# Running the stage ahead of each norm in two token halves, with the first half's norm steps issued inside the second half

## The reference

```python
h = h + (gate_a * ya + gate_b * yb) @ w_out                  # first model: two attentions
h = h + memory_cross_attn(rms_norm(h), rms_norm(mem), ...)
h = h + conv_gated_mlp(rms_norm(h), w_up, ..., w_down)       # 1024 -> 2*2816 -> 1024
x = rms_norm(h)                                              # ln_f: its result is the second model's input

# second model, each sublayer f: h = h + rms_norm_post(f(rms_norm_pre(h)))
#   layer 0: swiglu, gmlp_mixer, swiglu, embedding
#   layer 1: swiglu, rwkv7_mixer, swiglu, embedding
swiglu(x)    = (silu(x @ w1) * (x @ w3)) @ w2                 # D_FF 2816
embedding(x) = sigmoid(x @ w_gate) * (p @ w_proj)             # p: 512 x 256
rms_norm(x)  = x * rsqrt(mean(x*x, axis=-1) + 1e-6) * g
```

## Time and profile before

| | |
|---|---|
| median of 3 runs | 4235.42 us (4219.64 to 4237.18) |
| the profiled execution's own time | 4230.84 us |
| its span, first to last instruction | 4229.0 us |
| mean granted TensorE clock | 0.889 of full speed |
| busy: TensorE 87%, VectorE 44%, ScalarE 28% | of the span |
| HBM read / written | 279.07 MB / 2.10 MB |

### The profile page before, as it was taken

The page is one execution under the profiler, slowest core; times in us unless marked ns, Lnnn a source line. Parts: engine busy times, 40 slices in busy tenths (PEclk is TensorE's granted clock), DMA queues, the critical chain, the costliest instruction groups (busy, mean ns, idle before and its releaser), DMA issues. The chain is left out here.

```text
span 4229.0 us, 50513 instructions
## 1 busy us (share of the span) xinstructions
PE 3670.3 (87%) x22482; PEld 2958.7 (70%) x22482; DVE 1851.5 (44%) x2268; ACT 1167.1 (28%) x1423; POOL 0.2 (0%) x4
## 2 busy tenths in 40 slices
PE   7888579779998999869899978999687677689996
PEld 6656357658877887868788867887466666478874
DVE  5222223547734333454433244333646774743334
ACT  2222432332222222323322223222333231232222
POOL 0000000000000000000000000000000000000000
PEclk9758789869998999889899988999888987789997
DMA  3001012202222222212122311222120000012221
GB/s 134 30 0 60 0 50 100 70 30 100 93 90 77 100 84 95 100 50 100 60 100 88 102 65 60 100 85 66 62 78 28 3 3 12 31 69 100 85 90 40
DMA packets 43273, 284.40 MB, mean 67 GB/s; under 512 B 4785, under 2 KB 4913, under 8 KB 16817
## 3 DMA queue, kind: packets, MB, share of 16 engines
q1 hardware_dynamic: 43056, 281.18, 19.3%
HBM read 279.07 MB, written 2.10 MB: 66 GB/s over the span
## 5 line engine op out<-in xcount | busy, mean ns | idle before, releaser
L392 PE MATMUL ps<-xh,wh 128*128 128x512 f32 x2688 | 1065.2, 396 | 68.1 <-DVE xl L1502 33.9
L392 PE MATMUL ps<-xl,wh 128*128 128x512 f32 x2688 | 1059.6, 394 | 0.0
L392 PE MATMUL ps<-xh,wl 128*128 128x512 f32 x2688 | 1058.2, 394 | 0.0
L289 DVE TENSOR_TENSOR wl<-raw,wh 128x2048 fp32r<-128x2048 f32 (+3 forms) x284 | 591.6, 2083 | 557.7 <-ACT wh L284 556.7
L392 PEld LDWEIGHTS ps<-xh,wh 128*128 128x128 f32 x2688 | 511.7, 190 | 202.2 <-issue 83.5
L284 ACT CAST wh<-raw 128x2048 fp32r<-128x2048 f32 (+3 forms) x284 | 493.0, 1736 | 417.8 <-PE ps L392 412.6
L392 PEld LDWEIGHTS ps<-xh,wl 128*128 128x128 f32 x2688 | 511.3, 190 | 110.0 <-issue 1.5
L392 PEld LDWEIGHTS ps<-xl,wh 128*128 128x128 f32 x2688 | 512.3, 191 | 107.8 <-issue 0.8
L392 PE MATMUL ps<-hid_h,wh 128*128 128x512 f32 x880 | 347.1, 394 | 1.1 <-DVE wl L289 1.1
L392 PE MATMUL ps<-hid_h,wl 128*128 128x512 f32 x880 | 347.0, 394 | 0.0
L392 PE MATMUL ps<-hid_l,wh 128*128 128x512 f32 x880 | 347.0, 394 | 0.0
(11 more groups left out here) (301 smaller groups left out, 4025.8 us busy)
## 6 DMA issues: line engine op xcount, KB each, us to landing
raw<-in_up SPq DMA_DIRECT2D x88, 1024.0 KB, 4.9
raw<-in_down SPq DMA_DIRECT2D x64, 704.0 KB, 4.1
raw<-in_up_c SPq DMA_DIRECT2D x22, 1024.0 KB, 4.9
raw<-in_down_c SPq DMA_DIRECT2D x16, 704.0 KB, 4.0
raw<-in_gates SPq DMA_DIRECT2D x8, 1024.0 KB, 4.8
raw<-in_gv SPq DMA_DIRECT2D x8, 1024.0 KB, 4.9
raw<-in_gu SPq DMA_DIRECT2D x8, 1024.0 KB, 4.9
raw<-in_gout SPq DMA_DIRECT2D x8, 1024.0 KB, 4.9
```

The costliest lines, as they stand in the source:

```text
L289: nc.vector.tensor_tensor(wl[:, slot, 0:w], raw[:, slot, 0:w], wh[:, slot, 0:w].bitcast(F32), ALU.subtract).then_inc(lo_ready, 1)
L392: last = nc.tensor.matmul(out, stationary, moving, start=(fresh and q == 0), stop=(t == kt - 1 and half == per - 1 and q == 2), skip_group ...
```

## The change

The stages `down_c`, `down_00`, `down_01`, `down_10`, `down_11`, `gout`, `rout` and `ple_gate0/1` each run twice, as `...a` on tokens 0 to 255 and `...b` on tokens 256 to 511. Each half streams, casts and subtracts all the stage's weight chunks again. The stages behind the norms (`up_*`, `gv`, the rwkv inputs) stay whole.

A `Chain` holds the two passes of one token half as 12 numbered steps. `Chain(0)` is handed to stage b as `along`: at every hook (one a chunk in `down_*`, two a chunk in `gout`, `rout` and `ple_gate`) each engine issues its part of the next step, in line with the stage's own instructions: behind the split of the next chunk on ScalarE and VectorE, behind the chunk's matmuls on TensorE. What is left (`rest()`), and all of `Chain(1)`, is issued behind stage b, ahead of the next stage. In a chain the second pass's squares are added by VectorE and not by TensorE.

`embed` now runs `ple_proj` first (the split of `p` is made a whole feed-forward earlier), with `Chain(1)` of the norm ahead as its `along` and that of `ple_gate_a`; `ple_gate_b` carries `Chain(0)` of the next norm. The output leaves in two DMAs.

Everywhere a unit has at most two output tiles: `branch_a`, `branch_b`, `xo`, `lora_w2`, `lora_a2`, `lora_g2` and `ple_proj` evict two at a time where they evicted four, from 4 banks of PSUM by turns.

```diff
+def by_halves(name, width, count):
+    return [(name + "a", name, width, range(count)), (name + "b", name, width, range(count))]
...
+STREAM += stage("up_00", 2048, KF) + by_halves("down_00", DOWN, 2 * KD)
+STREAM += stage("gv", 2048, 8) + stage("gu", 2048, 8) + by_halves("gout", 2048, 8)
...
     def linear(...,
+               tokens=EVERY, last_rows=P, norms=None, sums=False, along=None):
+        hooks = max(1, blocks * kt // 8)
...
         @block.vector
         def _(dve):
...
+            for unit in range(units):
+                for half in range(per):
+                    n = a + unit // lots * per + half + 1
+                    if unit % lots == 0 and n < len(order):
+                        split_lo(dve, n, n % 2, order[n][2])
+                    if along:
+                        for _ in range(hooks):
+                            along.dve(dve, hook)
+                            hook += 1
+                if dve_part:
+                    wait_products(dve, unit)
+                    dve_part(dve, unit, outputs(unit), side(unit))
...
+    class Chain:
+        SUM, ROOT, APPLY, SUM_2, ROOT_2, WRITE, END = 0, 1, 2, 5, 6, 7, 12
+        def pe(self, pe, step):
+            if step == self.SUM:
+                self.one.sum_up(pe)
+            elif step == self.ROOT:
+                self.one.spread(pe)
+            elif step == self.SUM_2 and self.two:
+                self.two.sum_up(pe)
+            elif step == self.ROOT_2 and self.two:
+                self.two.spread(pe)
+        def act(self, act, step):
+            if step == self.ROOT:
+                self.one.square_root(act)
+            elif self.APPLY <= step < self.APPLY + 4 and self.two:
+                for t in range(2 * (step - self.APPLY), 2 * (step - self.APPLY) + 2):
...
+                    self.two.square(act, t, self.one)
...
+            elif self.WRITE <= step < self.WRITE + 4 and self.two and self.two.split:
+                for t in range(2 * (step - self.WRITE), 2 * (step - self.WRITE) + 2):
+                    self.two.high(act, t)
+        def dve(self, dve, step):
+            if step == self.ROOT:
+                self.one.invert(dve)
+            elif self.APPLY <= step < self.APPLY + 4:
+                t = 2 * (step - self.APPLY)
+                self.one.value(dve, t)
+                self.one.value(dve, t + 1)
+                self.one.finish(dve, t)
+                self.one.finish(dve, t + 1)
+                if self.two:
+                    if t:
+                        self.two.sum_squares(dve, t)
+                    self.two.sum_squares(dve, t + 1)
+            elif step == self.ROOT_2 and self.two:
+                self.two.invert(dve)
+            elif self.WRITE <= step < self.END and self.two:
+                t = 2 * (step - self.WRITE)
+                if t:
+                    self.two.finish(dve, t - 2)
+                    self.two.finish(dve, t - 1)
+                if t < KD:
+                    self.two.value(dve, t)
+                    self.two.value(dve, t + 1)
...
+    def down(name, move, target, tiles_made, *passes):
+        for half in range(2):
+            along = None
+            if half:
+                along = Chain(0, *passes)
+            linear(name + "ab"[half], HALF, P, hid_split, halves=True, norms=None if half else Made(tiles_made),
+                   along=along, **summing(move(HALVES[half]), target, 1, HALVES[half]))
+        return along
+    def up_onto(name, chain, *passes):
+        chain.rest()
+        other = Chain(1, *passes)
+        other.rest()
+        linear(name, KD, 256, x_split, norms=Ready(other), **swiglu())
...
+        other = Chain(1, *passes)
+        linear(f"ple_proj{layer}", 2, D, pt_split, norms=Ready(made), dve_part=to_tiles(proj, 2), along=other)
...
+        linear(f"ple_gate{layer}a", KD, 256, x_split, norms=Ready(chain), along=other, **gated(HALVES[0]))
+        other.rest()
+        along = Chain(0, *next_passes)
+        linear(f"ple_gate{layer}b", KD, 256, x_split, norms=Ready(other), along=along, **gated(HALVES[1]))
```

More of the change, by code:

```diff
@@ L132, in constants @@
     return {"const": c, "rope": rope, "dil": dil, "wmask": wm, "reset": reset}
[L136 to L145, removed]
+def stage(name, width, count):
+    return [(name, name, width, range(count))]
+def by_halves(name, width, count):
+    return [(name + "a", name, width, range(count)), (name + "b", name, width, range(count))]
@@ L148 @@
+STREAM += stage("rv", 2048, 4) + stage("lora_g2", 2048, 1) + by_halves("rout", 2048, 4)
+STREAM += stage("up_11", 2048, KF) + by_halves("down_11", DOWN, 2 * KD)
+STREAM += stage("ple_proj1", 2048, 1) + by_halves("ple_gate1", 2048, 4)
 class Steps:
@@ L334, in _, with wait_products @@
                     sp.wait_ge(lo_ready, n + 1)
[L335 to L349, removed]
-                    split_next(a + unit * per + half + 1)
-                if part:
-                    eng.wait_ge(chunks_used, a + unit * per + per + 2)
-                    part(eng, unit, outputs(unit), side(unit))
+                    load(sp, n + 2)
+        def wait_products(eng, unit):
+            if unit % lots < lots - 1:
+                eng.wait_ge(lot_done.sem, lot_done.after(unit // lots, unit % lots + 1))
+            else:
+                eng.wait_ge(chunks_used, a + unit // lots * per + per + 2)
         @block.scalar
@@ new lines, in finish, with dve @@
+        def finish(self, dve, t):
+            if self.onto:
+                self.add(dve, t)
+            elif self.split:
+                self.low(dve, t)
+        def dve(self, dve):
+            dve.wait_ge(chunks_used, self.multiplied)
+            dve.wait_ge(psum_read.sem, self.evicted)
+            if self.by == "vector":
+                for t in range(1, KD):
+                    self.sum_squares(dve, t)
+            self.invert(dve)
+            for t in range(KD):
+                self.value(dve, t)
+                if t:
+                    self.finish(dve, t - 1)
+            self.finish(dve, KD - 1)
@@ L726, in _ @@
     def _(sp):
[L727 to L728 removed]
+        load(sp, 0)
+        load(sp, 1)
         sp.dma_start(h[:, :, :], io["x"]).then_inc(loaded, 16)
@@ L1317, in gmlp @@
+    def gmlp(chain, passes, *next_passes):
         v = area("v", [P, TB, GW], 0)
@@ L1347, in gmlp @@
+        other = Chain(1, *passes)
+        other.rest()
+        linear("gv", KD, 256, x_split, norms=Ready(other), **gated_values(0))
         g_mean, g_sq, g_scale, g_root, g_done, g_mask, g_mix, g_bias = roles(
```

567 lines of the change are left out of this document (346 added, 221 removed).

## The result

| | before | after |
|---|---|---|
| median (4 runs each, side by side) | 4228.86 us (4219.64 to 4237.18) | 4268.06 us (4259.53 to 4277.44) |
| the profiled execution | 4230.84 us | 4259.53 us |
| its span | 4229.0 us | 4257.7 us |
| HBM read | 279.07 MB | 357.71 MB |

The ratio of after to before is 1.0094, 95% interval 1.006 to 1.0128: slower by 0.9%, that is by 39 us in the medians and 29 us between the two profiled executions. 4303 was forecast, 4238 to 4355 given as the range.

The account below looks back on a forecast made before the run. TensorE was taken as the bound, busy 3670 of 4229 us, with the winnable time in the waits between stages. 4230.8 - 78 + 20 + 33 + 91 + 7 = 4304, left at 4303 us; 8-in-10 range 4238 to 4355.

Parts of the forecast that it names:

- The term that decides, steps inside stage b: Stages b of down, gout, rout: norm steps and weight splitting take turns in two queues, delaying TensorE; 91 us lost.
- The hand-stepped list for down_b: Stage b of down: its 16 chunks stepped with traced durations, 4.0 to 8.2 us each; 79 us against 66 for stage a.
- the two-step chunk: Stage b of gout, two norm steps a chunk: the third listed chunk was to take 14.8 us.
- Splitting twice: Down, gout, rout halves: weights cast and subtracted again, each cast behind the old unit's copy and square; 33 us lost.
- spacing: Down and gout matmuls on 256 tokens: 120 ns each, a pair 6.7 ns more than one before; 20 us lost.
- the two rows: Matmul spacings of gv, 120 ns, and xv, 113 ns; the first taken for down and gout, the second for rout and gates.
- Waits: Between stages: only the second token half's chain remains, many waits falling from 30.9 to 20.0 us; 78 us gained with embeddings and evictions.
- giving up TensorE's sums: Waits between stages: dropping the squares summed by TensorE, 13.8 us in one wait, was called most of the gain.
- Evictions by two tiles: Ends of branch_a, branch_b, xo and lora_g2: two tiles in place of four spare two 0.69 us instructions; about 7 us gained.
- embedding blocks: Ple_proj first, gate by halves: layer 0 falls from 133.8 to 129.5 us, the last from 129.1 to 109.5.
- The clock: Inside stages b: two or three waits long enough to lower the granted clock; 7 us lost, between 0 and 20.
- The rival of a clock low through all steps: Stages b: clock stays low through the steps, 85 us for five down stages, some 15 for gout and rout; about 4400, chance 0.07.

Follow-up runs that it names:

- the first experiment: The changed kernel with no norm step inside stage b of down, gout and rout, the first half's norm running serially behind it; 4330.59 us, ratio 1.0246.
- the fifth: The changed kernel with ScalarE's step parts one step later, plus evictions behind the next unit's first cast and serial chains summed by TensorE; 4217.69 us, ratio 0.9988.
- seventh: The kernel of the fourth with norms ahead of up_00, up_01, up_10 and up_11 as whole-width chains, second pass summed by VectorE; 4179.06 us, one run.
- the third run: The kernel before with only the change's rewritten stage helpers, evicting two tiles at a time, every stage whole; 4197.24 us, ratio 0.9937.
- the fourth: The kernel of the third run with ple_proj ahead of a whole gate stage and the whole-width norm's steps along it; 4180.07 us, ratio 0.9896.

## Why the prediction was right, and where it was off

- **Direction and size.** Faster waits were outspent by longer stages, by the mechanism named. 4268 lies 35 us under the forecast; against the profiled execution, 4259.5, it is 44.
- **The term that decides, steps inside stage b: 91 us forecast, 85 measured** (changed kernel against the first experiment, seven stages). The 85 contain what the forecast had as a term of its own: 131 matmuls of the stages b ran at the low clock, none in the first experiment's, 13 us. The queues alone cost some 72. The hand-stepped list for down_b, 4.5, 4.5, 4.0, 5.0, 6.5, 8.2, 5.0, 4.0, ..., came out as 4.17, 4.24, 4.08, 4.70, 6.16, 7.78, 5.69, 4.07, ...: stage b 76.4 us against 79. Stepping a queue from durations in the trace gave each chunk within 0.7 us. In gout the two-step chunk, 14.8 by the list, took 14.6; rout was 9 us longer than forecast (70.7 against 61.5), by its first chunk above all, see the next point.
- **Splitting twice: 33 us, and spacing: 20 us. Together 53, measured 51** by the first experiment (10.5, 7.7, 6.0, 6.0, 6.7 for the downs, 3.9 gout, 10.4 rout). That they agree so well is in part luck: the five downs took 37 us where 46 were forecast, rout 10.4 where 4 were. The mechanism (a cast behind the old unit's copy and square) is shown by the fifth. A second mechanism was missed: the first chunk of a half is half the work, but its last input, or the weights behind it, come no sooner. Rout's first chunk took 13.05 us, as long as at full width (13.14), waiting for the last tile of the head norm; down_c's took 8.92 for 8.94. That is 7 and 5 us of the 51.

```profile
3682.56 0.39 PE L427 MATMUL ps<-xh,wh 128*128 128x256 f32 x1 [2.54 <-DVE xl L2373]
```

- The spacing was right as a mean and wrong as a rule: matmuls of down and gout sit at 113 or 118 ns, changing from chunk to chunk (mean 114 to 115.5), and rout's at 120, so the two rows were given to the wrong stages. What picks the level stayed open.
- **Waits: 78 us forecast.** gv 19.94 for 20.0, up_00 17.2 for 18.5, the rwkv mixer 28.6 for 30.6, up_11 26.7 for 29.5: good to 10%. Up_01 took 22.8 for 20.0, and here a moved step was missed: the split of `p`, formerly behind the gate, now stands in both queues between the sum over partitions and the mean, and waits for its data.

```profile
2072.03 0.61 PE L590 MATMUL ps<-const,rs 128*128 128x1 f32 x4 [1.47 <-DVE rs L880]
2074.13 1.14 ACT L823 CAST pt_h<-pt 128x512 fp32r<-128x512 f32 x2 [2.62 <-DMA pt<-in_p]
2074.88 1.29 DVE L833 TENSOR_TENSOR pt_l<-pt,pt_h 128x512 fp32r<-128x512 f32 x2 [2.91 <-ACT pt_h L823]
2076.09 0.15 DVE L614 TENSOR_SCALAR stats<-ps 128x2 f32<-128x2 f32 x1
```

- **One sentence was wrong: that giving up TensorE's sums "is most of the gain".** The earlier trace rows show 13.8 us of them, but beside them VectorE scaled and added for 11.3. At 256 tokens TensorE's sums would have been shorter in five of six waits (fifth run), and at 512 VectorE's are no gain ahead of up_01 and up_11 (seventh). The sum of the prediction stood because it was added up instruction by instruction, not from that sentence.
- **Evictions by two tiles: about 7 us forecast, some 23 measured** where they act alone (the third run's places, 6.1 + 12.9 + 3.6). The uses counted, stages of the first model and lora_g2, came to 9.7 of them, near the forecast; ple_proj, with 6.5 us each, was left out because the change also moves it. The embedding blocks came out 8.5 and 5.4 us below their forecast; how much of that is the eviction was not traced.
- **The clock: 7 us forecast.** In the seven stages some 185 matmuls of 256 columns ran at 213 ns in place of 113: 18.5 us, inside the range given and over twice the term. The rival of a clock low through all steps did not come: in the stages b of down it fell once or twice a stage, for 15 to 22 matmuls, behind some of the holes of 1.7 to 3.3 us, and never in down_c's. The Trainium skill's TensorE: Matmul & The Clock Gate, HAM oscillation, describes waits between short bursts that put the clock back every time. That the clock falls behind a wait agrees; here it did not after every one, and it came back within the burst.
- The 44 us to the profiled execution are, rounded: stages 16 (with the 7 for the clock in the forecast), embeddings 14, waits 3, all other stretches 12 (19 gained, 7 forecast). In the last, 9 us are a clock that nothing in the change explains, beside the 4 of the first attention: of lora_g2's 48 matmuls 43 ran 22.0 us at 0.51 in the execution before, and all 48 in 14.3 at 1.00 in the one after.

```profile
3568.60:3590.60 22.00, 22.00 (x43) 11.43 (x42) 0.11 (x1) 0.00 (x0) 0.00 (x0) 0.51 0.14 48
```

```profile
3596.70:3611.00 14.30, 14.25 (x48) 7.69 (x48) 5.74 (x7) 0.00 (x0) 0.00 (x0) 1.00 0.21 73
```

The stage did so at full clock in most kernels here and at half clock in the third, though its code there is that of the fourth.

## What to carry to other kernels

Slack that a profile shows as a low busy share is usable only in the order of the queues: before giving an idle engine work inside another stage, step two or three chunks by hand and look for an instruction that waits for another engine ahead of one that the bottleneck needs; issuing that instruction one turn later was worth 38 us here. Test each part of a bundled change by itself: this one hid 45 us of gain behind some 84 us of loss. Halving a stage to shorten the wait behind it pays only where the wait saved (here 16 us behind down_10) exceeds the price of feeding the weights twice and of the steps (here 10 to 14 us a down stage even when repaired).

## What the runs showed of the hardware

- Behind a hole of 2.15 us in stage b of down_00 the granted clock fell to 0.60, behind holes of 2.03 us in down_01 and 2.17 us in down_10 it stayed at 1.00 through the next burst. In stage a of down_00, with holes of up to 1.24 us, it stayed at 1.00.
- 256-column matmuls of one shape run at three spacings, 113, 118 and 120 ns. Within a stage the level changes at a chunk's start; in the changed kernel's split stages there was always a hole of 0.15 us or more ahead of it, in the fifth run three times none (as 118 to 113 ns at 1179.17 us, in down_c's stage a).
- Twice the weight traffic (DMA share 0.50 in place of 0.28) did not lengthen the loads: 4.0 to 4.1 us a chunk of 704 KB before and after. Where units ran at 7.48 us (fifth run) one nevertheless came 1.05 us late for its cast.
- Code that no edit touched ran at another granted clock from execution to execution: the rwkv recurrence 370.4 us at 0.88 and 383.8 at 0.84, the first attention 183.2 at 0.59 and 178.9 at 0.62.
